# A depthwise convolution in 4 time phases by 32 channels, taken for pairs of tiles and laid out through HBM

## The chip, the cores and the metric

The kernel runs on the eight NeuronCores of one Trainium2 chip, one sequence of the batch on each; the cores exchange nothing. The time of a run is the device time of the slowest core, in microseconds (us). The engines of a core are named as in the profile: PE (matmuls), DVE (vector), ACT (scalar activations), POOL (here it only issues DMAs whose descriptors are made in software), SP (issues DMAs whose descriptors are made in hardware).

## What is computed

One decoder block over x of 4096 steps by 1024 channels per core, cut to what matters here:

```python
h = ada_rmsnorm(x, g_ffn1, sh1, sc1)                 # FFN1, width 2816
x = x + 0.5 * gt1 * swiglu_ffn(h, w_ffn1_in, w_ffn1_out)

h = ada_rmsnorm(x, g_mix, sh2, sc2)                  # the mixer
u_val, u_gate, u_x, u_y = split(h @ w_in, [512, 1024, 1536])
u = u_val * sigmoid(u_gate)                          # conv half, 512 channels
u = causal_depthwise_conv(u, conv_w, conv_b)         # 31 taps
y_conv = silu(layernorm(u, ln_g, ln_b))              # over the 512 channels
y_rnn = rglru_group(u_x, u_y, ...)                   # 4-tap conv, gates, scan over time
x = x + gt2 * (concatenate([y_conv, y_rnn]) @ w_out)

h = ada_rmsnorm(x, g_ffn2, sh3, sc3)                 # FFN2, like FFN1
x = x + 0.5 * gt3 * swiglu_ffn(h, w_ffn2_in, w_ffn2_out)
return ada_rmsnorm(x, g_final, f_shift, f_scale)
```

## The kernel before

Channels lie on the 128 partitions and time on the free axis, in 8 tiles of 512 steps. First FFN1 runs over all tiles in pairs and leaves its result in an HBM scratch tensor `xmid`. Then `mix_ffn2(t)` (line 701) does mixer and FFN2 of one tile after the other. Weights are held in HBM as bf16 "slabs" of 128x2048 (512 KB): `w1i` and `w1o` of FFN1, `win` and `wout` of the mixer, `dcw` of its convolution, `w2i` and `w2o` of FFN2. SP loads them through ten slab buffers; a matmul multiplies one 128x128 block of a slab with 512 or 256 columns.

The order of instructions is made at build time. Every operation is entered with its engine, an assumed duration, its buffers and a priority (mixer of tile t: 1000 + 10 t; FFN2: 1100 + 10 t; a lower number goes first). A list scheduler then simulates the engines and writes each engine's fixed program; at run time every engine only waits on semaphores in that order. FFN2 matmuls of earlier tiles thus lie between the mixer's steps. PSUM has 8 banks: a bank written by a matmul is free again when ACT or DVE has read it.

The 31-tap convolution runs on PE. Two time phases (even and odd steps) by 64 channels lie on the partitions of `ub`; for each of 8 channel groups 16 shifted 128x128 matrices, banded by phase, are multiplied with 256 columns and summed in PSUM, 128 matmuls for a tile. DVE writes `ub` straight from the gated product with a stride of 2 in 64x256 pieces (`stt`, line 423), and the result is written back to time order in 64x256 pieces by ACT or DVE. The layer norm over channels sums with 4 matmuls of 512 columns against a matrix of ones.

The steps of a tile in `mix_ffn2`, in the order in which they are entered: load `xmid`; norm; `ux` (32 matmuls) and its 4-tap convolution on DVE; the gated product (`gg`, `gv`: 64 matmuls, a Tanh on ACT); the gate matmuls (8 with `sb_gates`), 8 Tanh on ACT, then Exp, Ln, Exp and the scan; convolution and layer norm; `uy` (32 matmuls) with a Gelu; the output projection with `wout` (64 matmuls); FFN2 (352 matmuls with `w2i`, each pair of banks needing a Silu on ACT and a product on DVE; 176 with `w2o`). Helper lines that the profile shows: 447 all matmuls (`mms`), 405 ACT (`act`), 423 and 427 DVE (`stt`, `tt`), 454 all DMAs (`dma`).

## Time and profile before

| | |
|---|---|
| median of 3 runs | 2398.92 us (2398.41 to 2400.83) |
| the profiled execution's own time | 2398.92 us |
| span of its slowest core, first to last instruction | 2397.4 us |
| spans of the 8 cores | 2389.8 to 2397.4 us |
| PE, DVE, ACT, POOL busy | 2312.5, 1195.1, 929.5, 110.8 us |
| DMA engines busy, all queues | 65% of the span, 195 GB/s |

A row of the profile gives an engine, a source line of a helper and the tile names (`ps` is PSUM, `sb_c` a 128x512 fp32 buffer, `sb_h` a 128x512 bf16 buffer). "Idle before" is the time in which that engine waited for the instruction that is named. Matmuls overlap, so the time of one inside a stream is the distance from start to start and not the duration that its row shows.

### The profile page before, as it was taken

Reading aid. Unit: us, or ns where it says so; the run is one execution under the profiler, and the core shown is the slowest. Engines: PE = TensorE matmul, PEld = TensorE weight load, DVE = VectorE, ACT = ScalarE, POOL = GpSimd, SP = SyncE. Lnnn points to the kernel's source line nnn. Section 1 sums busy time; section 2 is a strip of 40 time slices with the busy share of each in tenths; the row PEclk is TensorE's granted clock in tenths of the full one; section 3 lists DMA queues with packets and bytes.
Section 4 is the critical chain, followed back from the end, with each engine's and each line's share of the span. In section 5 each row is a group of like instructions: output and inputs, shape, how many; then the busy total and the mean of one; then the engine's idle time right before and its main releaser. Section 6 shows DMA issues by size and latency. Waiting matters only on the chain.

```text
span 2397.4 us, 34922 instructions; the slowest of 8 cores (2389.8 to 2397.4 us)
## 1 busy us (share of the span) xinstructions
PE 2312.5 (96%) x11346; PEld 1110.4 (46%) x11346; DVE 1195.1 (50%) x2015; ACT 929.5 (39%) x1394; POOL 110.8 (5%) x213
## 2 busy tenths in 40 slices
...
GB/s 251 203 252 236 174 205 222 184 200 198 225 194 176 186 173 169 181 206 176 185 209 266 186 184 191 193 172 211 183 167 219 177 159 222 180 156 188 163 182 183
DMA packets 135106, 466.64 MB, mean 195 GB/s; under 512 B 16368, under 2 KB 18544, under 8 KB 134256
## 3 DMA queue, kind: packets, MB, share of 16 engines
q1 hardware_dynamic: 117216, 386.54, 49.0%
...
q14 instruction: 83, 0.68, 0.1%
...
## 4 chain that ended last, share of the span: by engine, by line
PE 87%; DVE 7%; DMA 2%; issue 2%; ACT 0%; SPq 0%; DVEq 0%; ACTq 0%; POOLq 0%
PE ps L447 87%; DVE sb_c L766 1%; DVE sb_c L427 1%; DVE sb_c L413 1%; DVE sb_c L423 1%; DMA xmid<-sb_c 1%; DVE sb_ub L423 1%; DMA sb_slab<-wmod 1%; DVE sb_h L427 1%; DMA sb_c<-x 1%; SPq L454 0%; DVE sb_c L433 0%; DMA sb_slab<-w1i 0%; ACT sb_c L405 0%; DVEq L113 0%
## 5 line engine op out<-in xcount | busy, mean ns | idle before, releaser
L447 PE MATMUL ps<-sb_h,sb_slab 128*128 128x512 bf16 (+1 forms) x10160 | 2178.0, 376 | 38.0 <-ACT sb_h L405 27.7
L447 PEld LDWEIGHTS ps<-sb_h,sb_slab 128*128 128x128 bf16 x10160 | 994.8, 98 | 1199.5 <-issue 47.0
L427 DVE TENSOR_TENSOR sb_h<-ps,sb_c 128x512 bf16<-128x512 f32 x352 | 241.8, 691 | 691.6 <-PE ps L447 634.8
L405 ACT ACTIVATE sb_c<-ps 128x512 f32<-128x512 f32 x400 | 236.9, 596 | 839.2 <-PE ps L447 827.8
L427 DVE TENSOR_TENSOR sb_c<-sb_c 128x512 f32<-128x512 f32 (+1 forms) x492 | 310.6, 673 | 94.4 <-ACT sb_c L405 77.2
L405 ACT ACTIVATE sb_c<-sb_c 128x512 f32<-128x512 f32 (+1 forms) x338 | 201.9, 614 | 277.7 <-DVE sb_c L423 241.1
L423 DVE SCALAR_TENSOR_TENSOR sb_c<-ps,sb_gth,sb_c 128x512 f32<-128x512 f32 (+1 forms) x136 | 97.4, 718 | 272.2 <-PE ps L447 272.2
L405 ACT ACT_TABLE_LOAD x102 | 130.9, 1283 | 225.3 <-PE ps L447 206.2
L405 ACT ACTIVATE sb_h<-sb_c,sb_modv,sb_gs 128x512 bf16<-128x512 f32 x158 | 114.9, 802 | 40.7 <-DVE sb_modv L427 23.9
L447 PE MATMUL ps<-sb_ub,sb_slab 128*128 128x256 bf16 x1024 | 115.1, 273 | 0.1
L504 DVE SCALAR_TENSOR_TENSOR sb_slab<-sb_slab,sb_crow 128x1024 f32<-128x1024 f32 x88 | 107.1, 1217 | 8.0 <-DMA sb_slab<-wmod 6.9
L447 PEld LDWEIGHTS ps<-sb_ub,sb_slab 128*128 128x128 bf16 x1024 | 99.9, 98 | 15.5 <-issue 0.7
L423 DVE SCALAR_TENSOR_TENSOR sb_c<-sb_ux,sb_vecs,sb_c 128x512 f32<-128x512 f32 x96 | 72.1, 751 | 10.3 <-DVE sb_c L423 0.5
L454 POOL DMA_DIRECT2D y<-sb_c x56 | 30.1, 540 | 1001.3 <-DVE sb_c L413 785.0
L427 DVE TENSOR_TENSOR sb_h<-sb_c 128x512 bf16<-128x512 f32 (+1 forms) x98 | 66.2, 676 | 14.9 <-ACT sb_c L405 11.5
L423 DVE SCALAR_TENSOR_TENSOR sb_c<-ps,sb_modv,sb_c 128x512 f32<-128x512 f32 x64 | 48.0, 750 | 51.0 <-PE ps L447 51.0
L447 PE MATMUL ps<-sb_h,sb_ones 128*128 128x512 bf16 (+1 forms) x98 | 37.1, 381 | 23.9 <-DVE sb_h L427 23.8
L423 DVE SCALAR_TENSOR_TENSOR sb_ub<-sb_c,ps 64x256 bf16<-64x256 f32 x128 | 53.8, 420 | 8.9 <-DVE sb_ub L423 0.5
L454 POOL DMA_DIRECT2D xmid<-sb_c x64 | 34.8, 544 | 368.0 <-DVE sb_c L423 351.6
L405 ACT ACTIVATE sb_c<-sb_c,sb_lam 128x512 f32<-128x512 f32 x64 | 50.1, 807 | 2.3
L413 DVE TENSOR_SCALAR sb_c<-ps,sb_vecs 64x256 f32<-64x256 f32 x94 | 44.9, 485 | 5.1 <-PE ps L447 1.4
L405 ACT ACTIVATE sb_c<-sb_c,sb_modv,sb_gs 128x512 f32<-128x512 f32 (+1 forms) x62 | 42.5, 759 | 0.9 <-DVE sb_c L427 0.9
...
## 6 DMA issues: line engine op xcount, KB each, us to landing
sb_slab<-b_w2i SPq DMA_DIRECT2D x176, 512.0 KB, 3.3
...
sb_c<-x SPq DMA_DIRECT2D x64, 256.0 KB, 8.7
```

The source lines that it names most:

```text
L405: return A("ACT", dur, lambda: (lambda o, i: (lambda h: [h.activation(out=o, in_=i, func=func, bias=bias, scale=scale)]))(out(), in_()), r ...
L413: f = lambda: (lambda o, a: (lambda h: [h.tensor_scalar(out=o, in0=a, scalar1=s1, scalar2=s2, op0=op0, op1=op1)]))(out(), in0())
L423: return A("DVE", dur, lambda: (lambda o, a, b: (lambda h: [h.scalar_tensor_tensor(out=o, in0=a, scalar=scalar, in1=b, op0=op0, op1=op1)]) ...
L427: return A("DVE", dur, lambda: (lambda o, a, b: (lambda h: [h.tensor_tensor(out=o, in0=a, in1=b, op=op)]))(out(), in0(), in1()), reads, wr ...
L447: return [h.matmul(o, lhsT=l, rhs=r, start=(first and i == 0), stop=(last and i == n - 1)) for i, (l, r) in enumerate(pr)]
L454: lambda: (lambda o, i: (lambda h: [h.dma_start(out=o, in_=i)]))(out(), in_()),
L504: return lambda h: [h.scalar_tensor_tensor(out=w, in0=w, scalar=1.0, in1=crow.ap, op0=ALU.mult, op1=ALU.mult, accum_out=o)]
L766: A("DVE", 1.3, lambda m=m, a=a, i=i, c=c: (lambda o, x0, x1: (lambda h: [h.tensor_tensor_scan(out=o, data0=x0, data1=x1, initial=hst[c].a ...
```

## The change

The convolution now has four time phases by 32 channels on the partitions: 16 channel groups, 9 shifts each, 256 columns, and those 256 columns are 128 steps of each of two tiles. So 144 matmuls serve a pair of tiles, where 256 did. All tensors of activations have their columns in phase order (four blocks of 128 steps); only the 4-tap convolution and the scan work in time order, by strided access (`by_time`).

A partition's data changes between the two layouts, and that goes through HBM: POOL writes the gated product to `useq` (one DMA of 128 KB for 128 channels), SP reads it back as `ub` (4 DMAs for a tile, 512 runs of 256 bytes each); after the layer norm POOL writes the result to `yseq` (4 DMAs of 32 KB for each of 8 blocks, so 32 for a pair), and SP reads it back (4 DMAs of 128 KB for a tile, 512 runs of 256 bytes each). The layer norm works on the pair, with 8 matmuls of 256 columns against `ones_ph`.

`mix_ffn2(t)` is split into `mix_in(t)`, `mix_conv(pair)`, `mix_out(t)` and `ffn2(t)`, entered as: `mix_in` of both tiles, `mix_conv`, `mix_out` and `ffn2` of the first tile, `mix_out` and `ffn2` of the second. `mix_in` begins with the gated product, and has `uy` ahead of the gate matmuls. `xmid` is loaded twice, in `mix_in` and in `mix_out`. The loads of `dcw` go from 64 to 36.

```diff
-        def mix_ffn2(t):
-            P.prio = 1000 + 10 * t if t else MIX0
-            gate_op = (last_in, anchors[-2][1])[t] if t < 2 else ffn_anchor[t - 2]
...
+        def mix_in(t, gate_op, prio):
+            xs = load_x(xm_dr, t, after=(gate_op,) * 8, lat=8.0)
+            hb = norm(xs, M_SC2, M_SH2, prio=prio)
+            h2 = t % 2
+            for c in range(4):
...
+                ut = new(p1, "ut")
+                stt(lambda ut=ut: ut.ap, lambda s=s: s.ap, 1.0, lambda bv=bv: bv.ap, ALU.add, ALU.mult, [s, bv], [ut])
+                d = u_dr[t][c]
+                dma("PL", lambda d=d: d.ap, lambda ut=ut: ut.ap, D_ROW, slot_sem(ut, "PL"), [ut], [d], lat=4.0)
+            src = u_d[512 * t:512 * t + 512, :].rearrange("(g c) n -> c g n", c=32)
+            for q in range(NPH):
+                dma("SP", lambda q=q: ub_t[32 * q:32 * q + 32, :, NSH - 1 + TN * h2:NSH - 1 + TN * h2 + TN],
+                    lambda q=q: src[:, :, TN * q:TN * q + TN], D_SMALL, lambda q=q: ub_sems[h2][q], u_dr[t], [ub[h2][q]], lat=5.0)
...
-                for hh in range(2):
-                    g = 2 * c + hh
-                    slab = load_slab("dcw", g, False)
-                    mms(bank, [(lambda s=s, slab=slab: slab.ap[:, s * 128:(s + 1) * 128], lambda s=s, g=g: ub_t[:, g, 15 - s:271 - s]) for s in range(16)],
-                        [slab, ub[g]], cols=256, sub=slice(256 * hh, 256 * hh + 256))
+        def mix_conv(pr):
+            slabs = [load_slab("dcw", r, False) for r in range(NSH)]
...
+                for e in range(2):
+                    g = 2 * j + e
+                    per = {}
+                    for sh in range(NSH):
+                        per.setdefault((g * NSH + sh) // 16, []).append(((g * NSH + sh) % 16, sh))
+                    keys = sorted(per)
+                    for k in keys:
+                        mms(bank, [(lambda k=k, m=m: slabs[k].ap[:, m * 128:(m + 1) * 128],
+                                    lambda sh=sh, g=g: ub_t[:, g, NSH - 1 - sh:NSH - 1 - sh + 2 * TN]) for m, sh in per[k]],
+                            [slabs[k], ub_halo] + ub[0] + ub[1], first=(k == keys[0]), last=(k == keys[-1]), cols=256,
+                            sub=slice(256 * e, 256 * e + 256))
...
+                    return lambda h: [h.dma_start(out=yc_d[rows[q]:rows[q] + 64, :].rearrange("(g c) n -> c g n", c=32),
+                                                  in_=src[32 * q:32 * q + 32]) for q in range(NPH)]
+                op = A("PL", 1.2, f, [b], [yc_dr[pr][j]], nbytes=D_ROW, sem=slot_sem(b, "PL"), lat=4.0)
+                op.parts = NPH
...
+        def mix_out(t, yr, gate_op):
+            pr, h2 = t // 2, t % 2
+            yc = []
+            for c in range(4):
+                b = new(p1, "yc")
+                src = yc_d[pr * NPH * 512:(pr + 1) * NPH * 512, TN * h2:TN * h2 + TN].rearrange("(q r) n -> r q n", q=NPH)
+                dma("SP", lambda b=b: by_phase(b.ap), lambda src=src, c=c: src[128 * c:128 * c + 128], D_SMALL, slot_sem(b),
+                    [yc_dr[pr][2 * c], yc_dr[pr][2 * c + 1]], [b], lat=5.0)
+                yc.append(b)
+            xs = load_x(xm_dr, t, after=(gate_op,) * 8, lat=4.0)
+            yb = yc + yr
...
-        for t in range(n_tiles):
-            mix_ffn2(t)
+        for pr in range(n_tiles // 2):
+            ta, tb = 2 * pr, 2 * pr + 1
+            mp = 1000 + 20 * pr if pr else MIX0
+            P.prio = mp
+            gates_ = (last_in, anchors[-3][1]) if pr == 0 else (ffn_anchor[ta - 2][4], ffn_anchor[ta - 2][18])
+            yrs = [mix_in(t, g, 940 if pr else MIX0 - 10 + t) for t, g in zip((ta, tb), gates_)]
+            mid_op = mix_conv(pr)
+            xs = mix_out(ta, yrs[0], mid_op)
+            ffn2(ta, xs)
+            P.prio = mp
+            xs = mix_out(tb, yrs[1], ffn_anchor[ta][-1])
+            ffn2(tb, xs)
```

Where the scheduler put the work is seen in the engines' programs, at three places.

**PE, the first mixer.** Before, from the last 32 convolution matmuls of tile 0 on. `sb_ones` are sums of a norm. Of the x106, 50 are with `w1o` (FFN1 of the last pair) and the last 56 are the output projection of tile 0; of the x30, 8 end that projection and 22 are with `w1o` again, as are all of the x104:

```order
L447 MATMUL ps<-sb_ub,sb_slab 128x256 x32
L447 MATMUL ps<-sb_h,sb_ones 128x512 x2
L447 MATMUL ps<-sb_h,sb_slab 128x512 x8
L447 MATMUL ps<-sb_h,sb_ones 128x512
L447 MATMUL ps<-sb_h,sb_slab 128x512 x8
L447 MATMUL ps<-sb_h,sb_ones 128x512
L447 MATMUL ps<-sb_h,sb_slab 128x512 x106
L447 MATMUL ps<-sb_h,sb_ones 128x512
L447 MATMUL ps<-sb_h,sb_slab 128x512 x30
L447 MATMUL ps<-sb_h,sb_ones 128x512
L447 MATMUL ps<-sb_h,sb_slab 128x512 x104
```

Now, from the convolution of the first pair on. The x22 and the x44 are the last matmuls with `w1o`; the x56 and the x8 are the output projection of tile 0, which reads `yseq`; the x136 are FFN2 of tile 0 with `w2i`:

```order
L461 MATMUL ps<-sb_ub,sb_slab 128x256 x99
L461 MATMUL ps<-sb_h,sb_slab 128x512 x22
L461 MATMUL ps<-sb_ub,sb_slab 128x256 x27
L461 MATMUL ps<-sb_h,sb_slab 128x512 x44
L461 MATMUL ps<-sb_h,sb_ones_ph 128x256 x8
L461 MATMUL ps<-sb_h,sb_slab 128x512 x56
L461 MATMUL ps<-sb_h,sb_ones 128x512
L461 MATMUL ps<-sb_h,sb_slab 128x512 x8
L461 MATMUL ps<-sb_h,sb_ones 128x512
L461 MATMUL ps<-sb_h,sb_slab 128x512 x136
```

Behind the layer norm's sums (`ones_ph`) the output projection now follows at once, and FFN2 follows at once behind the norm's sums; FFN1's matmuls that stood between these are ahead of them.

**ACT, the mixer of a tile in the middle of the span.** Before: the 8 Tanh of the gates (`sb_bah`), then Exp and Ln of the recurrence, then evictions of the convolution (`sb_vecs`); no Silu of FFN2 stands here:

```order
L405 ACTIVATE sb_ux<-ps 128x512 x4
L405 ACTIVATE sb_c<-ps 128x512 x4
L405 ACTIVATE sb_c<-ps,sb_bah 128x512 x8
L405 ACTIVATE sb_c<-sb_c,sb_lam 128x512 x3
L405 ACTIVATE sb_c<-sb_c 128x512
L405 ACTIVATE sb_c<-sb_c,sb_cst 128x512
L405 ACTIVATE sb_c<-sb_c,sb_lam 128x512
L405 ACTIVATE sb_c<-sb_c 128x512
L405 ACTIVATE sb_c<-sb_c,sb_cst 128x512
L405 ACTIVATE sb_c<-sb_c,sb_lam 128x512 x4
L405 ACTIVATE sb_c<-ps,sb_vecs 64x256 x2
```

Now, the first tile of a pair. The row `sb_c<-ps 128x512` behind the four `sb_lam` is the first Silu of FFN2 since the Gelus (`sb_h<-ps`):

```order
L419 ACTIVATE sb_h<-ps 128x512 x4
L419 ACTIVATE sb_c<-ps,sb_bah 128x512 x8
L419 ACTIVATE sb_c<-sb_c,sb_lam 128x512 x3
L419 ACTIVATE sb_c<-sb_c 128x512
L419 ACTIVATE sb_c<-sb_c,sb_cst 128x512
L419 ACTIVATE sb_c<-sb_c,sb_lam 128x512
L419 ACTIVATE sb_c<-sb_c 128x512
L419 ACTIVATE sb_c<-sb_c,sb_cst 128x512
L419 ACTIVATE sb_c<-sb_c,sb_lam 128x512 x4
L419 ACTIVATE sb_c<-ps 128x512
L419 ACTIVATE sb_c<-sb_c 128x512
L419 ACTIVATE sb_c<-sb_c,sb_cst 128x512
```

In the first tile of a pair no convolution follows the gates; PE has only `w2i` matmuls there, and their Silu now stands among the recurrence's Exp and Ln.

**POOL, from the last stores of `xmid` on.** Before, and then now:

```order
L454 DMA xmid<-sb_c 128x512
L454 DMA b_w2i<-w2i 16x16384 x10
L454 DMA xmid<-sb_c 128x512 x16
L454 DMA sb_slab<-w2o 128x2048 x12
L454 DMA y<-sb_c 128x512 x56
```

```order
L468 DMA sb_slab<-w2o 128x2048 x8
L895 DMA yseq<-sb_h 32x2x256 x32
L468 DMA y<-sb_c 128x512 x16
L468 DMA useq<-sb_h 128x512 x8
L895 DMA yseq<-sb_h 32x2x256 x32
L468 DMA y<-sb_c 128x512 x16
L468 DMA useq<-sb_h 128x512 x8
L895 DMA yseq<-sb_h 32x2x256 x32
```

POOL only stored `y` there; it now issues 32 DMAs in a row for the `yseq` of each pair and 8 for its `useq`.

## Rows read from the trace of the kernel before

**Rows 1.** The page: the span, and each engine's busy time, share and instructions.
```profile
span 2397.4 us, 34922 instructions; the slowest of 8 cores (2389.8 to 2397.4 us)
PE 2312.5 (96%) x11346; PEld 1110.4 (46%) x11346; DVE 1195.1 (50%) x2015; ACT 929.5 (39%) x1394; POOL 110.8 (5%) x213
```

**Rows 2.** Busy time by stretch: PE, PEld, DVE, ACT, POOL, then PE clock, DMA share, GB/s.
```profile
1400.00:1600.00 200.00, 198.23 (x982) 95.71 (x981) 120.18 (x201) 100.86 (x147) 4.32 (x8) 1.00 0.53 183
```

**Rows 3.** PE's waits from 100 us to the end: total us, times, longest.
```profile
PE ps L447 <- DVE sb_h L427: 15.7, 10, 10.4
PE ps L447 <- DVE sb_ub L423: 9.0, 8, 1.3
```

**Rows 4.** Timeline of PE, tile 2's mixer: start us, us, instruction.
```profile
1197.31 12.44 PE L447 MATMUL ps<-sb_ub,sb_slab 128*128 128x256 bf16 x112
1209.58 5.34 PE L447 MATMUL ps<-sb_h,sb_slab 128*128 128x512 bf16 x24
...
1223.19 25.20 PE L447 MATMUL ps<-sb_h,sb_slab 128*128 128x512 bf16 x116
1248.22 0.38 PE L447 MATMUL ps<-sb_h,sb_ones 128*128 128x512 bf16 x1
```

**Rows 5.** Groups of instructions by shape: busy us, mean ns of one, idle before.
```profile
L427 DVE TENSOR_TENSOR sb_c<-sb_c 128x512 f32<-128x512 f32 x468 | 301.5, 686 | 87.9 <-ACT sb_c L405 70.7 <-DMA xmid<-sb_c 13.1 <-DVE sb_c L417 1.0
L405 ACT ACTIVATE sb_c<-sb_c 128x512 f32<-128x512 f32 x320 | 194.5, 626 | 249.3 <-DVE sb_c L423 212.9 <-DMA sb_c<-x 11.8 <-DVE sb_c L433 11.2
L405 ACT ACT_TABLE_LOAD x102 | 130.9, 1283 | 225.3 <-PE ps L447 206.2 <-DVE sb_c L423 10.0 <-DMA sb_vecs<-vecs 3.2
L447 PE MATMUL ps<-sb_ub,sb_slab 128*128 128x256 bf16 x1024 | 115.1, 273 | 0.1
L423 DVE SCALAR_TENSOR_TENSOR sb_ub<-sb_c,ps 64x256 bf16<-64x256 f32 x128 | 53.8, 420 | 8.9 <-DVE sb_ub L423 0.5
L423 DVE SCALAR_TENSOR_TENSOR sb_c<-ps,sb_modv,sb_c 128x512 f32<-128x512 f32 x64 | 48.0, 750 | 51.0 <-PE ps L447 51.0
L405 ACT ACTIVATE sb_c<-ps,sb_cst 128x512 f32<-128x512 f32 x31 | 21.3, 687 | 6.4 <-PE ps L447 6.1
L454 POOL DMA_DIRECT2D b_w2i<-w2i x22 | 10.8, 490 | 218.9 <-PE ps L447 218.9
L405 ACT ACTIVATE sb_c<-sb_c,sb_modv,sb_gs 128x256 f32<-128x256 f32 x13 | 6.6, 588 | 0.9 <-DVE sb_c L427 0.9
L405 ACT ACTIVATE sb_c<-ps,sb_cst 128x256 f32<-128x256 f32 x2 | 0.9, 474 | 1.1 <-PE ps L447 1.1
```

**Rows 6.** Timeline of POOL at 2164 us: five DMAs in a row.
```profile
2164.57 2.66 POOL L454 DMA_DIRECT2D y<-sb_c x5 [1.04 <-ACT sb_c L405]
```

**Rows 7.** DMA: a queue's packets, MB, share; then issues, KB each, median us to landing.
```profile
q1 hardware_dynamic: 117216, 386.54, 49.0%
xmid<-sb_c POOLq DMA_DIRECT2D x64, 256.0 KB, 3.0
sb_c<-xmid SPq DMA_DIRECT2D x64, 256.0 KB, 6.8
y<-sb_c SPq DMA_DIRECT2D x16, 128.0 KB, 1.8
```

**Rows 8.** Timeline of PE behind the norm of FFN1's second pair.
```profile
237.28 8.02 PE L447 MATMUL ps<-sb_h,sb_slab 128*128 128x512 bf16 x28 [10.35 <-DVE sb_h L427]
```

**Rows 9.** Busy time by stretch behind that wait, columns as in Rows 2.
```profile
237.00:241.00 4.00, 3.71 (x9) 1.31 (x10) 2.20 (x4) 0.65 (x1) 1.54 (x3) 0.50 0.68 267
241.00:244.00 3.00, 3.00 (x15) 1.36 (x14) 0.74 (x1) 0.00 (x0) 0.64 (x2) 1.00 0.68 127
```

**Rows 10.** Timeline of ACT, tile 2's gates and recurrence.
```profile
1194.98 4.73 ACT L405 ACTIVATE sb_c<-ps,sb_bah 128x512 f32<-128x512 f32 x8 [1.35 <-PE ps L447]
1199.73 1.28 ACT L405 ACT_TABLE_LOAD   x1
...
1208.33 3.32 ACT L405 ACTIVATE sb_c<-sb_c,sb_lam 128x512 f32<-128x512 f32 x4
```

More of the change, by code:

```diff
@@ L64, in __init__, with emit @@
         self.self_sync = self_sync
-def emit(eng, fn, reads=(), writes=(), dma=None, toks=()):
+def emit(eng, fn, reads=(), writes=(), dma=None, toks=(), parts=1):
     waits = {}
@@ L115, in replay @@
         if is_dma:
[L116 removed]
+            for x in ins:
+                x.then_inc(sem.h, 16)
         else:
@@ L166 @@
     __slots__ = ("eng", "dur", "fn", "reads", "writes", "prio", "tset", "deps", "succ", "ndep", "ready",
-                 "idx", "nbytes", "sem", "slab", "end", "after", "sync", "tok", "alt", "on", "lat")
+                 "idx", "nbytes", "sem", "slab", "end", "after", "sync", "tok", "alt", "on", "lat", "parts")
     def __init__(self):
@@ L391, in build_program @@
         ux = [fixed(f"ux{c}", [128, T + 3]) for c in range(4)]
-        ub_t = sb("ub", [128, 8, 271], BF16)
-        ub = [VB(ap=ub_t[:, g, :]) for g in range(8)]
+        UW = NSH - 1 + 2 * TN
+        ub_t = sb("ub", [128, 16, UW], BF16)
+        ub = [[VB(ap=None) for q in range(NPH)] for h in range(2)]
+        ub_halo = VB(ap=None)
+        ub_sems = [[newsem(f"s_ub{h}{q}") for q in range(NPH)] for h in range(2)]
+        ones_ph = fixed("ones_ph", [128, 128], BF16)
         cst = fixed("cst", [128, 2])
@@ L437, in cp, with mms @@
             return A("DVE", dur, lambda: (lambda o, i: (lambda h: [h.tensor_copy(out=o, in_=i)]))(out(), in_()), reads, writes)
-        def mms(bank, pairs, reads, first=True, last=True, cols=512, sub=None, prio=None):
+        def mms(bank, pairs, reads, first=True, last=True, cols=512, sub=None, prio=None, after=()):
             n = len(pairs)
@@ L460, in build_program, with slot_sem, f @@
         scr = {k: [VB(ap=dr(w_scr[k], r)) for r in range(w_scr[k].shape[0] // 128)] for k in w_src}
-        slot_sem = lambda b, q="SP": (lambda: b.pool.sems[q][b.slot])
+        def slot_sem(b, q="SP"):
+            def f():
+                if b.pool is p1:
+                    return ring[q][ring_at[q].__next__() % len(ring[q])]
+                d = b.pool.sems[q]
+                if b.slot not in d:
+                    d[b.slot] = newsem(f"s_{b.pool.name}{q}{b.slot}")
+                return d[b.slot]
+            return f
+        ring = {q: [newsem(f"s_ring{q}{i}") for i in range(10)] for q in ("SP", "PL")}
+        ring_at = {q: itertools.count() for q in ring}
+        in_ring = {id(x) for v in ring.values() for x in v}
         def load_slab(nm, r, cast, prio=None, after=(), sync=(), lat=6.0):
@@ new lines, in mix_conv @@
+                cv.append(v)
+            A("DVE", 0.3, lambda: (lambda h: [h.tensor_copy(out=ub_t[:, :, 0:NSH - 1], in_=ub_t[:, :, 2 * TN:2 * TN + NSH - 1])]),
+              ub[1], [ub_halo])
+            bank = new(ps, "ln")
+            sums = [[], []]
+            for hf in range(2):
+                for kind in range(2):
+                    acc = None
+                    for n, v in enumerate(cv[4 * hf:4 * hf + 4]):
+                        q = v
+                        if kind:
+                            q = new(p2, "cvsq")
+                            o, i = (lambda q=q: q.ap), (lambda v=v: v.ap)
+                            act(o, i, AF.Square, [v], [q], alt=v_sq(o, i))
+                        if acc is None:
+                            acc = q
+                            continue
+                        d = new(p1, "lnb") if n == 3 else (acc if kind else new(p2, "lna") if n == 1 else acc)
+                        tt(lambda d=d: d.ap, lambda q=q: q.ap, lambda acc=acc: acc.ap, ALU.add, [q, acc], [d])
+                        acc = d
+                    sums[kind].append(acc)
```

211 lines of the change are left out of this document (108 added, 103 removed).

## The prediction

> **What bounds the kernel now.** I read the page's busy table first, then busy time by stretch, then PE's waits, then timelines of the mixer. PE is busy for 2312.5 of 2397.4 us [rows 1], and in the middle of the span for 198.2 of each 200 us, at full clock, with DVE at 60%, ACT at 50% and the DMA engines at 53% [rows 2]. From 100 us to the end PE waits only 15.7 + 9.0 us for anything, 10.4 of it in one place [rows 3]. So the program is a stream of matmuls; a change pays by what it takes out of the stream and costs what holes it makes. DVE, ACT and DMA count only where PE must stand for them.
>
> **What is removed.** From start to start 112 convolution matmuls take 1209.58 - 1197.31 = 12.27 us, 0.1096 us each, and 116 matmuls of 512 columns take 25.03 us, 0.2158 each [rows 4]; the 0.273 us of the grouped row is one matmul's own length [rows 5]. The convolution goes from 1024 to 4 x 144 = 576 matmuls: 448 x 0.1096 = 49.1 us less. The layer norm's sums go from 32 of 512 columns to 32 of 256: 32 x 0.106 = 3.4 us less. Together **-52.5 us**. This is nearly certain.
>
> Small waits at the gate matmuls (9.0 us) and at norm sums (15.7 less the 10.4) can go too [rows 3], 14.3 us at most. The gate matmuls now stand behind `uy`, but DVE's chain for the fourth `ux` block has not become shorter, so I take **-4**, bounds -14 and 0.
>
> **What costs nothing, and what covers it.** The `ub` writes fall from 128 x 0.42 us [rows 5] to 32 of full height, some 0.72 each; evictions halve in number; four more adds of 0.69 us come for each tile. DVE and ACT have some 80 us of idle time in each 200 [rows 2], so I take nothing. The strided accesses also cost nothing: DVE's 64x256 write of `ub` already reads with a stride of 2 in 0.42 us. DMA bytes: 64 more loads of `xmid` (16.8 MB), four passes of 4.2 MB through `useq` and `yseq`, 28 slabs (14.7 MB) fewer, net +19 MB on 467, against engines 53% busy.
>
> The trip through `useq`: behind the last gated product PE has 32 + 32 + 6 matmuls, 15.1 us, before the convolution. In that time run Tanh and product (1.5 us), a POOL issue (0.53 us, 2.66 / 5 [rows 6]), a store (3.0 us, as `xmid` [rows 7]) and four loads by SP (1.8 us for 128 KB of 1 KB packets, 6.8 for a bunch of `xmid` loads [rows 7]): 7 to 12 us. No wait, 3 us to spare at worst. SP stands in its queue until the store has landed, and three `dcw` loads stand behind it, whose matmuls come 10 us into the convolution.
>
> **What it adds, first: the trip through `yseq` in the first pair.** In PE's program of the first pair nothing stands between the layer norm's sums and the output projection, which reads `yseq`. From the end of the sums: two evictions and a subtraction of 256 columns, Ln and Exp, each near 0.47 us, a multiply of 0.69, the load of the Silu table 1.28, two Silu of 0.59 [rows 5], sum 5.5, with the semaphores between eight steps some 7 us. Then POOL issues 32 DMAs at 0.53 us: 17.1 us (0.49 is its shortest issue [rows 5]: 15.7). The last lands 3.0 us after its issue began (6.8 at the worst), SP issues a load (0.3) and it lands. No row shows 256-byte packets. Below, the 128 KB store's 1.8 us; above, the mean time of a packet of SP's queue: 49.0% of 16 x 2397 us over 117216 packets is 0.16 us, so 32 packets on each engine take 5.1 us more, 6.9 [rows 7]. They are a thirteenth of the mean packet of 3.3 KB, so I take 3.0, nearer to the lower end. Sum 7 + 17.1 - 0.5 + 3.0 + 0.3 + 3.0 = **+30 us** of idle PE, bounds 25 and 38. The scheduler assumes 1.2 us of POOL for four of these DMAs (the `1.2` in the diff); the rows give 2.1.
>
> The sums themselves: behind the convolution PE has 44 matmuls, 9.5 us, while DVE has 12 adds of 0.69 and its part of the evictions and the scan. I take **+2**, bounds 0 and 5.
>
> The Trainium skill, page "DMA: Bandwidth & Descriptors", section "Anatomy of one DMA — SWDGE (gpsimd) path", gives a DMA 2.0 us plus its bytes at 436 GB/s; by that the last store and load would take an estimated 2.1 and 2.3 us, and the wait would be 1.6 us shorter. The Trainium skill says there too, under "Rules for kernel authors", that transfers under 64 KB are mostly overhead, which speaks against stores of 32 KB; no run here shows a transfer so small.
>
> **Second: a norm without cover.** After the output projection of tile 0 comes FFN2's norm, with only the sum's matmuls in between, where before matmuls of FFN1 stood. Its chain: 0.75 for the last residual add, square 0.63, add 0.69, sum 0.38, table 1.28, Ln 0.69, Exp 0.63, eight multiplies 5.5, the last scale 0.8 [rows 5], 11.4 us, with hand-overs **+12.5**. The trace has one such hole, 10.35 us beside partial cover [rows 8]; bounds 10 and 14.
>
> **Third: slow restarts.** Behind that 10.35 us hole the granted clock stood at 0.50, 1.2 GHz, for 4 us and then at 1.00 [rows 9], which costs 2 us. Two holes: **+4**, bounds 2 and 6.
>
> **Fourth: Silu behind the recurrence.** In the first tile of a pair PE has only `w2i` matmuls after the gates. Each pair of banks waits for a Silu, and ACT's program puts the next Silu behind 8 Tanh, 12 Exp and Ln and two table loads. Before, that row of work took 1194.98 to 1211.65 [rows 10]; with a table load and the Silu 18.6 us, about 19.0 from the first gate matmul. PE has 8 banks: 8 gate matmuls, one block of eight and four pairs of blocks, 1.7 + 1.7 + 13.8 = 17.2 us. It stands 1.8 us; then one Silu frees one pair (3.45 us) while ACT goes back for four Ln and Exp and two table loads, 6.3 us, and it stands 2.9. That is 4.7 in each of three pairs (the first pair fills with FFN1's output, which needs no Silu): **+14**, bounds 0 (ACT's steps pack more tightly than beside the convolution) and 25.
>
> In pairs 1 to 3 the `yseq` trip has cover: 162 matmuls of other tiles, 35 us, stand between the sums and the projection in pairs 2 and 3, 246 in pair 1. 30 us fit.
>
> **Sum.** -52.5 - 4 + 2 + 30 + 12.5 + 4 + 14 = +6 us. The profiled execution took 2398.92 us, which is the median too (its span is 1.5 us less): 2398.9 + 6 = **2405 us**, 0.25% slower. All lower bounds together give 2369 us, all upper ones 2434; taken as independent, the uncertain terms spread the sum by some 12 us either way.
>
> **Rivals.**
> *Faster.* The Silu waits do not appear, because the Tanh, Exp and Ln take less time without the convolution's evictions between them. For it: the trace's ACT waits for DVE within that work, and DVE is relieved. Against it: the table loads stay. The place is PE in the first tile of pairs 1 to 3; the price is 14 us, giving 2391. It decides below 1 us for each pair.
> *Small packets.* At 0.16 us for each of 32 packets on an engine, the eight loads of a pair take 8 x 5.1 = 41 us and POOL's 17 no longer set the pace. The seventh load, the last that tile a needs, lands 7 + 4.3 + 3 + 7 x 5.1 = 50 us after the sums: 20 us more in the first pair, 15 over the 35 us of cover in two others, 2455 us in all. For it: the mean packet. Against it: that mean carries 3.3 KB. The Trainium skill, page "DMA: Bandwidth & Descriptors", section "Why small descriptors are slow (HBM only)", puts the loss of a 256-byte descriptor at 27%; by that this rival would not occur, and no row here shows it.
> *No change.* The holes of the first pair are as forecast, and the Silu waits are half as long, 7 us: 2398 us. For it stands that ACT has idle time beside the recurrence; against it that the order of its program is fixed.
>
> **How the numbers follow.** The forecast, and cases a little above it, that end slower by over 0.2%: 0.43. Small packets or another wait in every pair: 0.07. No change, within 0.2% (4.8 us, about what a measurement of this kernel can tell): 0.26. Faster: 0.24. The range reaches from 2388 (the Silu waits and 3 us more of the small ones gone) to 2428 (the first pair's holes and the Silu waits at their upper ends); the forecast's own range is 2400 to 2415.
>
> **What would show it.** Right: PE's busy time near 2260 us; 576 convolution matmuls; one hole of near 30 us and one of near 10 close together around 1000 us, the first released by a load of `yseq`, with the clock at 0.50 behind each; 32 POOL issues at 0.53 us each; in each later pair waits of some 5 us for ACT before `w2i` matmuls. Wrong: POOL issues shorter than 0.4 us, matmuls of FFN2 waiting for slab loads that stand behind SP's `yseq` loads, or a wait at each convolution for `useq`.

## The result, and the profile after

The changed kernel took 2425.11 us (median of 4 runs; 2399.88 for the kernel before on the same chip): 1.0101 times as long, 95% interval 1.0078 to 1.0124, so 25 us or 1.0% slower. In some executions of any kernel here the cores of one die run at a lower granted clock; those are left out of all ratios. A time in us of an experiment below is its ratio to the kernel before, measured on the same chip, times 2398.9; in this measure the change itself takes 2423 us.

The page of the profiled execution (2425.48 us): span, busy time, then two groups of section 5; the `ux` group is from the groups by shape, whose columns are those of [rows 5].

```profile
span 2423.9 us, 34181 instructions; the slowest of 8 cores (2398.0 to 2423.9 us)
PE 2262.1 (93%) x10694; PEld 1068.8 (44%) x10898; DVE 1145.5 (47%) x1866; ACT 924.6 (38%) x1397; POOL 196.6 (8%) x374
L895 POOL DMA_DIRECT2D yseq<-sb_h x128 | 67.6, 536 | 138.8 <-ACT sb_h L419 135.8
L461 PE MATMUL ps<-sb_ub,sb_slab 128*128 128x256 bf16 x576 | 65.0, 273 | 1.4 <-ACT sb_c L419 1.4
L419 ACT ACTIVATE sb_ux<-ps 128x512 f32<-128x512 f32 x32 | 35.3, 1103 | 33.6 <-PE ps L461 33.6
```

Against [rows 1], PE has 50.4 us less work and the span is 26.5 us longer: PE stands 161.8 us where it stood 84.9. The waits of PE on core 0, the slowest, over the whole span (columns as in [rows 3]):

```profile
PE ps L461 <- DMA sb_h<-yseq: 37.9, 3, 30.1
PE ps L461 <- ACT sb_h L419: 37.3, 2, 28.4
PE ps L461 <- DVE sb_h L441: 31.4, 8, 11.7
PE ps L461 <- ACT sb_c L419: 10.9, 10, 2.4
PE ps L461 <- DMA sb_slab<-b_w2i: 10.9, 2, 8.6
PE ps L461 <- DVE sb_ux L451: 4.3, 5, 1.2
PE ps L461 <- DMA sb_slab<-w2o: 1.0, 1, 1.0
```

28.4 us for ACT and 23.7 for DVE are the start of the program and FFN1's second pair, which the change leaves alone. The rest in its places, from the timeline of PE on core 0: the first pair (four rows), the first full pair, that is pair 1 (four), and pairs 2 and 3.

```profile
1052.49 0.60 PE L461 MATMUL ps<-sb_h,sb_ones_ph 128*128 128x256 bf16 x4 [0.64 <-DVE sb_h L441]
1083.19 13.79 PE L461 MATMUL ps<-sb_h,sb_slab 128*128 128x512 bf16 x54 [30.10 <-DMA sb_h<-yseq]
1101.89 0.38 PE L461 MATMUL ps<-sb_h,sb_ones 128*128 128x512 bf16 x1 [2.96 <-DVE sb_h L441]
1111.23 30.89 PE L461 MATMUL ps<-sb_h,sb_slab 128*128 128x512 bf16 x133 [8.97 <-ACT sb_h L419]
...
1204.04 3.61 PE L461 MATMUL ps<-sb_h,sb_slab 128*128 128x512 bf16 x16 [1.45 <-ACT sb_c L419]
1210.04 27.79 PE L461 MATMUL ps<-sb_h,sb_slab 128*128 128x512 bf16 x125 [2.38 <-ACT sb_c L419]
...
1342.13 2.16 PE L461 MATMUL ps<-sb_h,sb_slab 128*128 128x512 bf16 x6 [2.38 <-DMA sb_slab<-b_w2i]
...
1362.90 3.57 PE L461 MATMUL ps<-sb_h,sb_slab 128*128 128x512 bf16 x8 [8.56 <-DMA sb_slab<-b_w2i]
...
1571.96 10.52 PE L461 MATMUL ps<-sb_h,sb_slab 128*128 128x512 bf16 x47 [2.32 <-ACT sb_c L419]
...
1701.69 13.64 PE L461 MATMUL ps<-sb_h,sb_slab 128*128 128x512 bf16 x55 [3.34 <-DMA sb_h<-yseq]
...
1915.84 12.21 PE L461 MATMUL ps<-sb_h,sb_slab 128*128 128x512 bf16 x47 [2.33 <-ACT sb_c L419]
...
2048.33 13.93 PE L461 MATMUL ps<-sb_h,sb_slab 128*128 128x512 bf16 x55 [4.43 <-DMA sb_h<-yseq]
```

The two holes of the first pair stand where and as long as they were forecast. Two kinds of wait have no counterpart in the sum: `w2i` slabs in pair 1, and `yseq` in pairs 2 and 3. The slab waits stand on all eight cores (8.3 to 12.8 us); the later waits for `yseq` do not: core 0 has 7.8 us of them, core 3 (2398.0 us) 0.5 and core 4 (2401.3 us) none. No core waits for `useq`. The forecast's sum against core 0:

| term | forecast | found |
|---|---|---|
| matmuls removed | -52.5 | -52.5 by count; PE's busy time, -50.4, holds the slow restarts and lacks 204 of 10898 matmul records |
| small waits, sums | -4 + 2 | -4 (14.3 before [rows 3]; 10.1 now: the waits from 300 us on that have no line of their own here) |
| first pair, `yseq` | +30 | +30.1 |
| first pair, norm | +12.5 | +11.9 (2.96 + 8.97) |
| slow clock behind these two | +4 | +3.2 |
| Silu behind the recurrence | +14 | +8.5 (1.45 + 2.38, 2.32, 2.33); other waits for ACT +2.4 |
| slabs in pair 1 | 0 | +11.9, and some 2 of slow clock |
| `yseq` in pairs 2 and 3 | 0 | +7.8, and 3.4 of slow clock |
| sum | +6 | +25 (span: +26.5) |

The slow clock is told from two views. By stretch (columns as in [rows 2]), the granted clock behind the 30 us hole is 0.50, which is 1.2 GHz, and 1.00 (2.4 GHz) from 1087 us:

```profile
1083.00:1085.00 2.00, 1.81 (x5) 0.70 (x5) 0.00 (x0) 0.00 (x0) 0.00 (x0) 0.50 0.02 4
...
1087.00:1089.00 2.00, 2.00 (x11) 0.87 (x9) 0.79 (x2) 0.63 (x1) 0.00 (x0) 1.00 0.00 0
```

And the 56 projection matmuls behind it take 13.79 us, where 56 x 0.2158 is 12.1: 1.7 lost. The 136 behind the norm lose 1.5, the 56 behind the waits of 3.34 and 4.43 us 1.6 and 1.8.

Where the 30.1 us go, from the timelines of POOL and SP on core 0. The first three rows are the first pair; the others are pair 3, whose sums end at 2008.9 us:

```profile
1060.51 8.85 POOL L895 DMA_DIRECT2D yseq<-sb_h  x16 [5.11 <-ACT sb_h L419]
1069.77 8.41 POOL L895 DMA_DIRECT2D yseq<-sb_h  x16 [0.41 <-issue]
1066.08 15.16 SPq L468 DMA_DIRECT2D sb_h<-yseq  x8
...
2016.82 0.56 POOL L895 DMA_DIRECT2D yseq<-sb_h  x1 [53.55 <-ACT sb_h L419]
...
2026.57 8.42 POOL L895 DMA_DIRECT2D yseq<-sb_h  x16 [0.91 <-ACT sb_c L419]
...
2042.08 1.25 SPq L468 DMA_DIRECT2D sb_h<-yseq  x2
```

First pair: 7.4 us from the end of the sums (1053.1) to POOL's first issue, 17.7 of POOL, 3.1 to the end of SP's last load issue, 1.9 until it lands. Pair 3: 7.9, 18.2, then 8.3 from POOL's end to the end of SP's last issue and 5.0 to land: 39.4 us. POOL takes as long; both landings take far longer. The DMA engines are busier there: their share is 0.34 from 1078 to 1083 us and 0.91 from 2035 to 2048 us, where `w2i` slabs are loaded and POOL has issued eight stores of `y`.

### The profile page after: what moved, and what is told of

Its sections match the earlier page's. It is cut to its first block, busy times and chain, and to the rows that moved or that the text cites. A ratio compares the mean times of both kernels' runs of the same rounds, so it can differ in the third digit from the quotient of the medians.

```text
span 2423.9 us, 34181 instructions; the slowest of 8 cores (2398.0 to 2423.9 us)
## 1 busy us (share of the span) xinstructions
PE 2262.1 (93%) x10694; PEld 1068.8 (44%) x10898; DVE 1145.5 (47%) x1866; ACT 924.6 (38%) x1397; POOL 196.6 (8%) x374
## 4 chain that ended last, share of the span: by engine, by line
PE 77%; DMA 6%; DVE 5%; ACT 5%; issue 3%; POOL 1%; SPq 1%; DVEq 0%; ACTq 0%; POOLq 0%
PE ps L461 77%; ACT sb_c L419 4%; DVE sb_c L441 3%; DMA sb_slab<-w1i 2%; POOL yseq L895 1%; SPq L468 1%; ACT L419 1%; DMA xmid<-sb_c 1%; DVE sb_h L441 1%; DMA b_w2o<-sb_slab 1%; DMA yseq<-sb_h 1%; DMA sb_slab<-b_w2i 1%; DVE sb_c L813 1%; DMA sb_slab<-wmod 1%; DVE sb_c L437 1%
## 5 line engine op out<-in xcount | busy, mean ns | idle before, releaser
L419 ACT ACTIVATE sb_c<-ps 128x512 f32<-128x512 f32 (+1 forms) x392 | 229.7, 592 | 823.5 <-PE ps L461 797.3
L441 DVE TENSOR_TENSOR sb_c<-sb_c 128x512 f32<-128x512 f32 (+1 forms) x524 | 332.5, 674 | 107.0 <-ACT sb_c L419 86.7
L419 ACT ACTIVATE sb_h<-sb_c,sb_modv,sb_gs 128x512 bf16<-128x512 f32 x166 | 120.2, 802 | 46.6 <-DVE sb_modv L441 24.6
L895 POOL DMA_DIRECT2D yseq<-sb_h x128 | 67.6, 536 | 138.8 <-ACT sb_h L419 135.8
L461 PE MATMUL ps<-sb_ub,sb_slab 128*128 128x256 bf16 x576 | 65.0, 273 | 1.4 <-ACT sb_c L419 1.4
L441 DVE TENSOR_TENSOR sb_h<-sb_c 128x512 bf16<-128x512 f32 (+1 forms) x82 | 55.5, 677 | 21.5 <-ACT sb_c L419 17.1
L461 PEld LDWEIGHTS ps<-sb_ub,sb_slab 128*128 128x128 bf16 x576 | 56.1, 98 | 11.2 <-issue 3.2
L437 DVE SCALAR_TENSOR_TENSOR sb_h<-sb_c,ps 128x512 bf16<-128x512 f32 x32 | 21.7, 686 | 65.5 <-PE ps L461 49.3
L468 POOL DMA_DIRECT2D useq<-sb_h x32 | 17.3, 542 | 418.5 <-DVE sb_h L437 417.0
L419 ACT ACTIVATE sb_ux<-ps 128x512 f32<-128x512 f32 x32 | 35.3, 1103 | 33.6 <-PE ps L461 33.6
```

The source lines that it names most:

```text
L419: return A("ACT", dur, lambda: (lambda o, i: (lambda h: [h.activation(out=o, in_=i, func=func, bias=bias, scale=scale)]))(out(), in_()), r ...
L437: return A("DVE", dur, lambda: (lambda o, a, b: (lambda h: [h.scalar_tensor_tensor(out=o, in0=a, scalar=scalar, in1=b, op0=op0, op1=op1)]) ...
L441: return A("DVE", dur, lambda: (lambda o, a, b: (lambda h: [h.tensor_tensor(out=o, in0=a, in1=b, op=op)]))(out(), in0(), in1()), reads, wr ...
L461: return [h.matmul(o, lhsT=l, rhs=r, start=(first and i == 0), stop=(last and i == n - 1)) for i, (l, r) in enumerate(pr)]
L468: lambda: (lambda o, i: (lambda h: [h.dma_start(out=o, in_=i)]))(out(), in_()),
L895: return lambda h: [h.dma_start(out=yc_d[rows[q]:rows[q] + 64, :].rearrange("(g c) n -> c g n", c=32), in_=src[32 * q:32 * q + 32]) for q ...
```

## Experiments

**1. The `w2o` casts moved into FFN1.** In the program the twelve `w2o` slabs are read in fp32, cast and written back when tile 0's FFN2 output comes, in pair 1.

```diff
-        prep = [(nm, r) for nm in ("win", "dcw", "wout", "w2i") for r in ...]
+        prep = [(nm, r) for nm in ("win", "dcw", "wout", "w2i", "w2o") for r in ...]
-                    slabs = [load_slab("w2o", 3 * q + s, t == 0 and cs.start == 0) ...]
+                    slabs = [load_slab("w2o", 3 * q + s, False) ...]
```

> The twelve w2o slabs are cast to bf16 in HBM while FFN1 runs, as those of w2i are, and no longer on the way of FFN2's first tile; nothing else is edited. Theory: the hole of 10.9 us before w2i matmuls in the first full pair, with the 1.0 us for w2o and the slow clock behind it, comes from DMA engines that are full there because w2o is read in fp32, cast and written back; it goes, and the time is 2425 - 12 to 17 = 2408 to 2413 us. Rival A, SP's queue (the slab loads stand behind yseq loads that wait for POOL): the hole stays at 8 us or more and the time within 5 us of 2425. Rival B, the 256-byte packets of useq and yseq fill the engines by themselves: the DMA share in that stage stays near 1.0 and the hole stays.

Measured: 1.0164 [1.0125, 1.0202], 2438 us. That is not faster than the change, and rather slower; by how much is loosely known, since the executions counted run from 2427.72 to 2453.53 us and the interval only just misses that of the change. The slab waits are gone (0.6 us), but FFN1, where the DMA share of core 0 was 0.83 already in the change (400 to 600 us), has new waits, and in pair 1 a wait for `yseq` appears, which the slab waits may have hidden. The timeline of PE on core 7:

```profile
477.37 0.58 PE L461 MATMUL ps<-sb_h,sb_ones 128*128 128x512 bf16 x1 [6.82 <-DVE sb_h L441]
...
1376.69 13.73 PE L461 MATMUL ps<-sb_h,sb_slab 128*128 128x512 bf16 x56 [6.50 <-DMA sb_h<-yseq]
...
1719.11 14.88 PE L461 MATMUL ps<-sb_h,sb_slab 128*128 128x512 bf16 x56 [7.07 <-DMA sb_h<-yseq]
```

So the casts do make the slabs late, but DMA time is scarce in FFN1 too.

**2 and 3. One store for a block, and then the first tile's loads first.** `yseq` gets rows in the order group, phase, channel, so that one DMA writes a block; a load then takes four DMAs.

```diff
-                    return lambda h: [h.dma_start(out=yc_d[rows[q]:rows[q] + 64, :]..., in_=src[32 * q:32 * q + 32]) for q in range(NPH)]
+                    dst = yc_d[r0:r0 + 256, :].rearrange("(g p) n -> p g n", p=128)
+                    return lambda h: [h.dma_start(out=dst, in_=src)]
```

In the second run the loads of the second tile are also ordered behind the last load of the first:

```diff
-                op = A("SP", 0.06, f, ..., lat=5.0)
+                op = A("SP", 0.06, f, ..., lat=5.0, after=(yc_last.get(pr),) if h2 else ())
```

> yseq is laid out so that one DMA of 128 KB writes a block where four of 32 KB did: POOL issues 8 instead of 32 for a pair; SP reads a block with 4 DMAs of 32 partitions instead of one. The 256-byte packets stay as many. Theory of the prediction (POOL's issue at 0.53 us sets the pace of the first pair's hole): the chain becomes 5.5 us of layer norm, 8 blocks at 1.4 us of DVE, a last Silu, 0.5 issue, 3 to land, 1.2 of SP's issues and 3 to land, some 22 to 24 us, so the hole of 30.1 falls to 21 to 24 and the waits of 3.3 and 4.4 us for yseq in the two last pairs go: time 2425 - 12 to 16 = 2409 to 2413. Rival, small packets set the pace of the trip: the hole stays within 2 us of 30 and the time within 5 of 2425.

> As the run with one store of 128 KB for a block, but SP issues all loads of the pair's first tile ahead of those of its second, where it took turns. In that run POOL was done 16.5 us after the sums and PE still waited 26.3, while SP issued 32 loads one after the other at 0.475 us. Theory (POOL's issues set the first pair's hole, and when they are fewer SP's issues of the second tile's loads do): the hole is 16.5 us and, from the start of the last store's issue, 3.0 to land, four issues of SP at 0.475 and 2.0 to land, 22 to 24 us in all. Rival (the 256-byte packets land late whatever the order): 25 us or more. The time falls by the same 2 to 4 us against that run, within what can be told.

Measured: 1.0093 [1.0079, 1.0107], 2421 us, a miss, since this can't be told from the 2423 us of the change; and 1.0064 [1.0045, 1.0083], 2414 us. The hole of the first run (PE and SP, core 7) and that of the second (PE, core 0):

```profile
1087.77 13.63 PE L461 MATMUL ps<-sb_h,sb_slab 128*128 128x512 bf16 x56 [26.27 <-DMA sb_h<-yseq]
1072.40 15.20 SPq L909 DMA_DIRECT2D sb_h<-yseq  x32
```

```profile
1077.84 13.62 PE L461 MATMUL ps<-sb_h,sb_slab 128*128 128x512 bf16 x56 [21.30 <-DMA sb_h<-yseq]
```

With 8 issues POOL is done 16.5 us after the sums (ACT's 16 Silu at 0.6 us now set its pace), yet PE waits 26.3: SP issues 32 loads without a pause, 0.475 us each, those of both tiles in turn. With the first tile's loads ahead the hole is 21.3, a little under the 22 to 24 expected, with as many 256-byte packets. The number of DMA issues on the path set this hole, first POOL's, then SP's, and not the size of the packets.

**4 and 5. Cover for the first pair out of the pair itself.** First the second tile's output projection is let go with the first's; then its `ux`, `uy` and gate matmuls go behind the convolution as well.

```diff
-            xs = mix_out(tb, yrs[1], ffn_anchor[ta][-1])
+            xs = mix_out(tb, yrs[1], ffn_anchor[ta][-1] if pr else mid_op)
...
+            if t in (1,):
+                P.prio = 805
             xr, xrb = [], []
```

> In the first pair the output projection of the second tile is let go with that of the first, so that its 64 matmuls (13.8 us) can stand beside the norm of FFN2 of the first tile; nothing else is edited. Theory (the 2.96 + 8.97 us hole behind the first projection is a chain without cover): it falls to some 2 to 4 us, the slow clock behind it goes, time 2425 - 8 to 12 = 2413 to 2417; the 30 us hole stays. Rival, the time is lost to whichever work comes later (the moved matmuls are missing as cover in the first full pair): time within 5 us of 2425.

> As the run before, and in the first pair the recurrence half of the second tile (ux, uy, gate matmuls, 72 of them, 15.6 us) gets a priority behind FFN1's last matmuls, so that the convolution goes ahead of it and it stands beside the yseq trip. Theory: the hole of 30 us falls by the 12 to 15 us of matmuls that now lie in it, in pieces; with the norm's hole the time is 2425 - 20 to 28 = 2397 to 2405, no more than before the change. Rival, the DVE and ACT work of that tile's recurrence delays the layer norm's chain and the stores: the hole shrinks by less than 8 us, time 2406 or more.

Measured: 1.0051 [1.0035, 1.0067], 2411 us: the norm's hole falls from 11.9 to 2.5 us, as expected, and the time to a little below the range expected. Then 1.0030 [1.0018, 1.0042], 2406 us, at the edge: the hole of 30 us becomes waits of 5.84, 2.61 and 2.72 us for DVE's `ux` chain and 9.13 for `yseq`, so that 72 matmuls of cover, 15.6 us, gain 9.8. Half of the rival is true: these matmuls wait for DVE in their turn.

**6. Cover out of FFN1.** The first pair's mixer starts earlier, so that FFN1's last matmuls stand behind the sums.

```diff
-N_P2 = 40
-N_P1 = 62
+N_P2 = 36
+N_P1 = 70
-            gates_ = (last_in, anchors[-3][1]) if pr == 0 else ...
+            gates_ = (anchors[-9][1], anchors[-6][1]) if pr == 0 else ...
```

> Only the first pair's mixer starts earlier: the loads of its two tiles are let go nine and six steps before the end of FFN1's last pair instead of at its last w1i matmul and three steps before the end, and 8 bf16 buffers more (4 fp32 buffers fewer) hold FFN1's hidden blocks meanwhile. Then some 45 us of w1o matmuls stand behind the layer norm's sums and some 10 us ahead of FFN2's first norm's end. Theory (the holes of 30.1 and 2.96 + 8.97 us and the slow clock behind them cost 43 to 47 us because nothing covers them): both holes fall to under 5 us in sum and the time falls by 38 to 47 us, to 2378 to 2387, faster than before the change; the slab waits of the next pair stay. Rival (moving the cover only moves the hole, since the DMA engines or DVE are the limit there): less than 25 us gained, 2400 or more.

Measured: 0.9900 [0.9883, 0.9916], 2375 us: 48 us off, and faster than before the change. The timeline of PE on core 5, with no wait from the sums to FFN2's first matmuls:

```profile
990.88 1.04 PE L461 MATMUL ps<-sb_h,sb_ones_ph 128*128 128x256 bf16 x8
991.75 53.69 PE L461 MATMUL ps<-sb_h,sb_slab 128*128 128x512 bf16 x248
1045.28 0.38 PE L461 MATMUL ps<-sb_h,sb_ones 128*128 128x512 bf16 x1
...
1050.89 29.30 PE L461 MATMUL ps<-sb_h,sb_slab 128*128 128x512 bf16 x135
```

The slab wait of pair 1 stays (12.4 us on that core).

**7. The `w2o` casts spread over tile 0's `w2i` matmuls**, one cast for each of the first twelve slabs, on the change as it is.

```diff
+                if t == 0 and n < 12:
+                    dma("PL", lambda d=scr["w2o"][n]: d.ap, lambda n=n: dr(w_src["w2o"], n), ..., sync=(ops[-1],), prio=450 + n)
```

> The twelve w2o slabs are cast from HBM to HBM during FFN2's w2i matmuls of the first tile, where the DMA engines were half idle, instead of on the way of that tile's output; FFN1 is untouched. After the run that cast them during FFN1 (the slab waits went, and FFN1 and the yseq trip lost more than that), the theory is that the DMA engines' load at the wrong time costs, and that here there is room: the slab waits of 10.9 + 1.0 us go and nothing comes back in FFN1: time 2425 - 8 to 15 = 2410 to 2417. Rival 1: in pair 1 a wait for yseq of about 6.5 us appears in their place, as in that run, since the slab waits had hidden it; then 2416 to 2422. Rival 2: the casts delay the useq stores or the win slabs of the next pair, holes of 5 us or more there, and no gain.

Measured: 1.0253 [1.0238, 1.0268], 2460 us: rival 2, and worse than it. By stretch and from the timeline of PE on core 4:

```profile
1140.00:1160.00 20.00, 18.71 (x87) 8.29 (x85) 3.46 (x5) 2.80 (x5) 2.92 (x6) 1.00 1.05 130
1160.00:1180.00 20.00, 3.27 (x8) 1.02 (x8) 0.00 (x0) 0.00 (x0) 0.00 (x0) 0.66 1.02 128
```

```profile
1167.09 3.27 PE L461 MATMUL ps<-sb_h,sb_slab 128*128 128x512 bf16 x8 [8.38 <-DMA sb_slab<-b_w2i]
1193.50 0.58 PE L461 MATMUL ps<-sb_h,sb_ones 128*128 128x512 bf16 x1 [23.15 <-DVE sb_h L441]
```

While casts are in flight the engines are full at 130 GB/s; slabs come late, then the next tile's `xmid` (57.5 us to land, median), whose norm keeps PE for 23 us. My reading of a share of 0.5 as room for casts at that rate was wrong.

**8. Costs near the measured ones in the scheduler.**

```diff
-                op = A("PL", 1.2, f, [b], [yc_dr[pr][j]], ..., lat=4.0)
+                op = A("PL", 2.15, f, [b], [yc_dr[pr][j]], ..., lat=7.0)
-                    [yc_dr[pr][2 * c], yc_dr[pr][2 * c + 1]], [b], lat=5.0)
+                    [yc_dr[pr][2 * c], yc_dr[pr][2 * c + 1]], [b], lat=7.0)
```

> Only numbers of the scheduler: 2.15 us of POOL for four yseq stores instead of 1.2, landing times of 7 us each for yseq stores and loads instead of 4 and 5, near what the profile shows under load. It then puts 160 instead of 112 FFN2 matmuls between the layer norm's sums and the projection in the two last pairs. Theory: the waits of 3.3 and 4.4 us for yseq there (only on some cores) were too little cover for a trip that takes 39 us under DMA load and not 31; they go, and nothing else changes: time 2425 - 3 to 9 = 2416 to 2422. Rival: the trip grows with the work that is put in front of it (slab loads of those matmuls ahead of it in SP's queue), waits as before, within 3 us of 2425.

Measured: 1.0040 [1.0026, 1.0055], 2409 us. PE waits for `yseq` only in the first pair; 48 matmuls more ahead of the projection suffice. It gains more than expected, since in pair 1 too the work has moved and the slab waits fall from 10.9 to 6.6 us.

**9. The three together** (6, 7 and 8).

> The three edits of these runs together: earlier start of the first pair, w2o casts during FFN2 of the first tile, real costs. If the three causes are separate and the cover holds: 43 + 10 + 6 us off, 2425 to about 2366, range 2358 to 2378. If the DMA engines are the limit wherever the work is put: 2385 or more.

Measured: 0.9994 [0.9985, 1.0004], 2397 us. The cover holds, but the spread casts take it back: 19.38 us for a `w2i` slab at 1132 us and 12.27 for the norm behind it. The expectation counted on 10 us of gain from the edit of run 7, which costs 36; with the 48 of run 6 and the 15 of run 8 the three measured effects add up.

**10. The `w2o` cast left out**, on the kernel of run 8. FFN2's output reads rows of `w2i` in place of `w2o`, as many and as large, so the program computes something else; the casts and SP's write-backs of the cast slabs are gone.

```diff
-                    slabs = [load_slab("w2o", 3 * q + s, t == 0 and cs.start == 0) ...]
+                    slabs = [load_slab("w2i", 3 * q + s, False) ...]
```

> As the run with real costs, but the w2o cast is left out of the program: FFN2's output takes rows of the w2i scratch in place of w2o's, with the same number and size of slab loads, so that 12 reads of 1 MB in fp32 and 12 write-backs of 0.5 MB are gone (18 MB a core) and nothing takes their place. The output is not the reference's. Theory (the slab waits of the first full pair come from these 18 MB beside the xmid, y, wout, useq and yseq transfers): no wait for a slab above 1 us from 1200 to 1400 us, DMA share there 0.7 instead of 0.85, and the time falls from 2409 by 7 to 12 us, to 2397 to 2402. Rival (SP's queue: slab loads stand behind yseq loads that wait for POOL's stores): waits of 4 us or more before w2i matmuls stay, time within 4 us of 2409.

Measured: 1.0009 [0.9999, 1.0019], 2401 us, 7 less than run 8, as expected. From 1200 to 1400 us PE waits for no slab at all, with the same `yseq` loads in SP's queue: the slab waits come from the casts and not from the `yseq` loads. Landing times from 1300 to 1400 us (KB each, median us), the change and then this run (run 8 has 14.3 and 18.9):

```profile
sb_slab<-b_w2i SPq DMA_DIRECT2D x21, 512.0 KB, 11.4
sb_slab<-b_wout SPq DMA_DIRECT2D x4, 512.0 KB, 21.4
```

```profile
sb_slab<-b_w2i SPq DMA_DIRECT2D x27, 512.0 KB, 4.8
sb_slab<-b_wout SPq DMA_DIRECT2D x4, 512.0 KB, 4.7
```

The edit takes out two things at once: the casts' transfers, and twelve write-backs, which SP issues in the queue of the slab loads and which hold a slab buffer until they land. In the change both stand in the chain that ends at the longest slab wait (1362.90 us), here from the view of the chain that ended last (start us, us):

```profile
1327.15 18.22 DMA b_w2o<-sb_slab
...
1345.44 17.21 DMA sb_slab<-b_w2i
```

The slab is let go when a write-back has landed, 18 us after that was issued, and takes 17 us itself. Run 7, whose casts go from HBM to HBM without write-backs by SP, has a slab wait too (8.38 us), so the casts' transfers are enough to cause one; how the 11.9 us of the change divide between the two no run tells.

**11. Cover and real costs** (6 and 8), the best version.

> The earlier start of the first pair with the real costs of the scheduler, w2o cast as in the change. If the two effects add up (48 us for the cover, 8 to 15 for the costs), ratio to before 0.984 to 0.987, 2362 to 2369 us; if the costs only mattered through the places of the slab loads that the cover has moved too, within 4 us of the cover alone, 2372 to 2380.

Measured: 0.9843 [0.9830, 0.9856], 2361 us: the effects add up. It is 1.6% faster than the kernel before.

**12. Silu ahead of the recurrence**, on run 11.

```diff
-                act(..., AF.Silu, [bg], [s], tset=(SILU,))
+                act(..., AF.Silu, [bg], [s], tset=(SILU,), prio=1010)
```

> As the run before, and the Silu of FFN2 gets a priority ahead of the next pair's recurrence on ACT (1010 instead of 1100 and more). Theory (ACT's order makes PE wait 1.5 + 2.4 us for Silu in the first full pair and 2.3 in each later one): these waits go, table loads rise by some ten, and the time falls by 4 to 8 us against the run before. Rival: the Silu between the Exp and Ln delay the recurrence or the layer norm's chain, so that the waits only change their place: within 3 us of it.

Measured: 0.9906 [0.9874, 0.9939]; the median is 2373.32 us against 2362.34 of run 11 on the same chip, 11 us slower. The Silu waits go, and gates, layer norm and projection are late instead, as on core 0 in pair 2:

```profile
1572.01 12.25 PE L461 MATMUL ps<-sb_h,sb_slab 128*128 128x512 bf16 x56 [1.55 <-ACT sb_c L419]
1585.92 0.59 PE L461 MATMUL ps<-sb_h,sb_gates 128*128 128x512 bf16 x2 [0.80 <-DVE sb_ux L451]
1621.86 1.03 PE L461 MATMUL ps<-sb_h,sb_ones_ph 128*128 128x256 bf16 x8 [2.02 <-DVE sb_h L441]
```

With 4.36 and 2.17 us of the same kind in pair 1 these waits explain that it is no faster. Over the whole span PE's waits sum to 85.9 us on that core and to 80.3 on the slowest core of run 11, whose span is 9.1 us shorter; the mean granted clock is 0.991 against 0.993. How the rest divides I did not trace.

## Why the prediction was right, and where its size was off

The sign was right and the time lies in the range, 3 us below its upper end; the forecast itself was 20 us low. The holes of the first pair came as forecast, but the sign does not follow from them: the forecast's own terms, as found on core 0, sum to -0.4 us (-52.5 - 4 + 30.1 + 11.9 + 3.2 + 8.5 + 2.4), and the 25 us are two waits that the prediction had put at nothing. Run 10, in which neither is left, measures 1.0009 [0.9999, 1.0019], about the time before. That the change is slower, and that the range holds it, is thus in part luck: the range reached that far for longer holes and Silu waits.

- *What is removed*: 576 convolution matmuls as said; PE's busy time is 2262.1 us, near the 2260 named.
- *The trip through `yseq` in the first pair*: 30.1 us found, 30 forecast, and its parts too: 7.4 (7 forecast), 17.7 of POOL at 0.536 us each (17.1), 3.1 and 1.9 for the landings (3.0, 0.3 and 3.0, less 0.5). Run 6 shows that it costs time, runs 2 and 3 that the number of issues sets it, POOL's first. The other price of the load in the prediction, 2.3 us, is one for DMAs that POOL issues, and SP issues this one; the sum does not use it.
- *A norm without cover*: 11.9 found, 12.5 forecast; runs 4 and 6 remove it.
- *Silu behind the recurrence*: right in kind, too large: 1.45 and 2.38 us in pair 1 (1.8 and 2.9 forecast), but only one of 2.3 us in each of pairs 2 and 3, so 8.5 and not 14.
- *"30 us fit"* is the first step that failed. The cover of 35 us was right, the trip under load is not that of an empty stage: 39.4 us, since the landings take 13.3 and not 5.0 beside slab loads and `y` stores. I had taken the landings for the first pair and used the sum in the others. Run 8 shows that cover was lacking: with 48 matmuls more there is no wait.
- *"DMA bytes ... against engines 53% busy"* is the second. The share of one stretch in the middle was used for the whole, and for bytes alone. In pair 1 the `w2o` casts run. Before, twelve of them were issued from 1201 to 1250 us, and the engines were full for 100 us, with slab loads beside them and eight stores of `y` from 1285 us on; the change puts eight of them between 1284 and 1303 us, with `xmid`, `wout`, `useq`, `yseq` and `y` close behind. By stretch, the kernel before and the change (columns as in [rows 2]):

```profile
1200.00:1250.00 50.00, 49.55 (x282) 27.30 (x281) 39.17 (x66) 33.96 (x49) 6.36 (x12) 1.00 0.98 206
1250.00:1300.00 50.00, 50.00 (x233) 22.65 (x232) 23.88 (x37) 26.66 (x37) 4.32 (x8) 1.00 0.97 310
```

```profile
1300.00:1350.00 50.00, 46.10 (x220) 21.99 (x223) 41.39 (x65) 35.59 (x61) 21.94 (x41) 0.97 1.01 276
1350.00:1400.00 50.00, 41.09 (x181) 18.21 (x183) 12.24 (x18) 8.55 (x14) 0.00 (x0) 0.90 0.72 236
```

  Before, the full stage did no harm: PE was busy for 49.55 and 50.00 of 50 us there. My reading is that nothing urgent stood behind it. Run 10 shows the casts, with their write-backs, as the cause. The prediction had named `w2i` slabs that come late as a sign of error, but behind SP's `yseq` loads, which run 10 excludes; SP did stand, but for the casts (28.4 us from 1280 to 1370 us) and their write-backs (13.0).
- *Small packets* did not occur: loads of 128 KB in runs of 256 bytes landed in 2.7 us (median) in the first pair, where 0.16 us for each of 32 packets gives 6.9. The Trainium skill, page "DMA: Bandwidth & Descriptors", section "Why small descriptors are slow (HBM only)", speaks of a loss of 27% for 256 bytes; the trace agrees so far as such a loss is too small to be seen beside the landing. *Faster* fell with the Silu waits: it wanted less than 1 us for each pair, and 2.3 to 3.8 were found. *No change*, 2398 us, has the holes as forecast and 7 us of Silu waits; with 8.5 found it described these terms better than the forecast did, and fell only by the two steps above.

What stays open: how the slab waits divide between the casts' transfers and their write-backs, what the rest of run 12's loss is, and whether the 256-byte packets lengthen the landings under load, which no run here tells apart from the load of the slabs.
